# An output projection moved behind eight expert products on TensorE

## The chip, the cores and the metric

The kernel runs on one core of one Trainium2 chip. The metric is the device time of one execution in microseconds (us). Engines are named TensorE (PE in the rows), VectorE (DVE), ScalarE (ACT), GpSimd (POOL) and SyncE (SP); PEld is TensorE's loading of weights.

## What is computed

One layer over 512 tokens of width 1024, float32: a token mixer, then a mixture of single-neuron experts (PEER). The change lies where the one ends and the other begins. Cut to that:

```python
out = jnp.concatenate([y_conv, y_rwkv], axis=-1) @ w_out      # output projection
x = x + gt1 * _rmsnorm(out, ng[1])
hc = _modulate(_rmsnorm(x, ng[2]), sh2, sc2)
q = (hc @ wq).reshape(PEER_CHUNK, PEER_HEADS, 2, D_HALF)
s = jnp.einsum('chsd,hskd->chsk', q, subkeys)
vals, idx = lax.top_k(s, PEER_TOPK)
...                                                           # 16 experts for a token and head: ex, sc
g = jax.nn.softmax(sc.astype(jnp.float32), axis=-1)
act = jax.nn.gelu(jnp.einsum('chkd,cd->chk', u[ex], hc), approximate=False)
y = jnp.einsum('chk,chkd->cd', g * act, v[ex])
```

## The kernel before

The 512 tokens are four tiles of 128. For each tile there are 8 heads, and for each head and token 16 experts, so 32 heads in all (g counts them) with 16 products each. The work of a head goes like this. GpSimd gathers, for each expert slot j, the row of u of each token (128 rows of 4 KB) and the row of v into two rings of 8 buffers each (`gather`, L1570). VectorE multiplies each u row with the tokens and sums (the dots, L1908). When all sixteen dots of a head are there, ScalarE takes gelu of them (L1719), and VectorE multiplies with the softmax (`expert_w`, L1925). ScalarE then makes a diagonal matrix of each weight column (`diags`, L1623, 4 buffers), and TensorE adds diagonal times v row into two PSUM banks (`experts`, L1968, two matmuls of 512 columns, each of which has two records in the trace). The products of head g - 1 are made while the dots of head g run. Between the dots VectorE also chooses the experts of the next head.

The order on each engine is written out by hand in the body of `pool6`, `scalar6`, `vector6` and `tensor6`, and semaphores tie the engines. What sets it around the change:

- GpSimd gathers u row j of head g, then v row j of head g - 1, in turn. U row j waits until the dot that used its buffer 8 slots before is done (`dots`), v row j until the product that used its buffer is done (`experts_added`). A gather that waits holds back all behind it. In head 1 of tile 0 the v rows 8 to 15 of head 0 are gathered beside u rows 8 to 15 of head 1.
- TensorE in tile 0, head 1: after `mixer_moved` reaches 1, eight products of head 0; `project_out(3, 0)`, the output projection of token tile 3 into banks 0 and 1 (L553, 16 matmuls); eight more products. In head 2: `columns(1)`, `columns(2)` (L1437, transposes of the normed rows of tile 1 and 2 into banks 0 and 1; `columns(1)` waits for `mixer_moved` 3), the products of head 1, `columns(3)`. From head 3 on, queries and scores of the later tiles (`late_query` L1989, `late_scores` L1997) stand between the products.
- ScalarE in tile 0, head 1: diagonals 0 to 3, `square_outputs(2)` (L1308 to L1314: it moves the projection out of the banks, takes the sum of squares and a root, and raises `mixer_moved`), diagonals 4 to 7, `square_rows(2)` (L1319), diagonals 8 to 11, `square_outputs(3)`, diagonals 12 to 15; then `exps` (L1645) and gelu. In head 2: the staging of scores (L1616), `square_rows(3)`, `move_columns(1)`, `move_columns(2)` (L1329), the diagonals of head 1, `move_columns(3)`.
- VectorE: `norm_outputs(3)` (L1334 to L1340) stands behind the last dot of head 1 and waits for the root that `square_outputs(3)` makes. Behind it is the wait for gelu.
- SyncE: when all four projections are done (`mixer_output` 4) it loads the first two slices of wq, 1 MB each, for the late queries.

Of the kernel before, what the change touches and what calls it, by code (L numbers as in the profile page):

```python
# [71 lines left out]
def _layer(nc, stack, x, c, ctx_in, c_ctx, w_mod, b_mod, norm_gains, w_in, w_out, conv_w, tshift_mu,  # L72
# [224 lines left out]
    def v3(a):  # L297
        return a.rearrange("p (i c) -> p i c", c=P)
# [1227 lines left out]
    NSL = TOPK  # L1526
# [21 lines left out]
    def late_head(t, h):  # L1548

        if not isinstance(t, int) or t > 1:  # L1550
            return None
        n = h - 3 if t == 0 else h + 5
        return n if 0 <= n < HEADS else None
# [56 lines left out]
    def scalar6(act):  # L1610

        def stage_scores(t, h):

            g = t * HEADS + h
            first = isinstance(t, int) and t == 0
            nc.scalar.activation(SCs[:, h % 2], SC0[:, 2 * h:2 * h + 2, :] if first else SC[:, t, 2 * h:2 * h + 2, :],  # L1616
                                 ACT.Identity).then_inc(scores_staged, 1)

        def diags(g, hp, js):
            for j in js:  # L1620
                if not (isinstance(g, int) and g == 0 and j < 4):
                    act.wait_ge(experts_added, NSL * g + j - 3)
                nc.scalar.activation(diag[:, j % 4], ident, ACT.Identity, scale=expert_w[:, hp % 2, j:j + 1]).then_inc(weight_diagonals, 1)  # L1623

        def last_diagonals():

            act.wait_ge(expert_weights, LAST_HEAD + 1)
            for k, j in enumerate(MULTIPLIED):
                act.wait_ge(experts_added, NSL * LAST_HEAD + k - 3)
                nc.scalar.activation(diag[:, k % 4], ident, ACT.Identity,  # L1630
                                     scale=expert_w[:, LAST_HEAD % 2, j:j + 1]).then_inc(weight_diagonals, 1)

        def finish_last():
            t = NT - 1
            nc.scalar.activation(final_stats[:, 5:6], eps[:, 0:1], ACT.Sqrt)
            act.wait_ge(experts_added, PRODUCTS)
            nc.scalar.activation(tail_squares, psum_all[:, 6 * 512:8 * 512], ACT.Square, accum_out=final_stats[:, 0:1]).then_inc(final_scalar, 1)
            act.wait_ge(final_scalar, 3 * t + 1)
            nc.scalar.activation(final_stats[:, 3:4], final_stats[:, 0:1], ACT.Sqrt, bias=eps[:, 0:1], scale=1.0 / D).then_inc(final_scalar, 1)

        def exps(g):

            act.wait_ge(experts_chosen, g + 1)
            act.wait_ge(probabilities, 2 * g)
            nc.scalar.activation(prob, top, ACT.Exp, bias=neg_largest[:, 0:1], accum_out=exp_sum[:, 0:1]).then_inc(probabilities_raised, 1)  # L1645

        def finish(t):

            act.wait_ge(experts_added, NSL * HEADS * (t + 1))
            act.wait_ge(final_vector, 4 * t + 4)  # L1650
            nc.scalar.activation(square_dump[:, 0:512], PO[0][:, :], ACT.Square, accum_out=final_stats[:, 0:1]).then_inc(final_scalar, 1)
            act.wait_ge(final_scalar, 3 * t + 1)
            nc.scalar.activation(square_dump[:, 0:512], PO[1][:, :], ACT.Square, accum_out=final_stats[:, 1:2]).then_inc(final_scalar, 1)
            act.wait_ge(final_vector, 4 * t + 5)
            nc.scalar.activation(final_stats[:, 3:4], final_stats[:, 2:3], ACT.Sqrt, bias=eps[:, 0:1], scale=1.0 / D).then_inc(final_scalar, 1)


        def late_query(i):

            act.wait_ge(late_queries, i + 1)  # L1660
            nc.scalar.activation(qB[:, i % 2], LATE_QUERY_BANKS[i % 2][:, 0:3 * P], ACT.Identity).then_inc(late_queries_moved, 1)

        def late_scores(i):

            act.wait_ge(late_scores_done, i + 1)
            nc.scalar.activation(SC[:, 1:NT, i, :], v3(LATE_SCORE_BANKS[i % 2][:, 0:3 * P]), ACT.Identity).then_inc(late_scores_moved, 1)

        def body(t, first):
            for h in range(HEADS):
                g = t * HEADS + h  # L1670
                if h == 0 and not first:
                    act.wait_ge(dots, NSL * g)
                    nc.scalar.activation(h2cur, H2N[:, t, :], ACT.Identity).then_inc(h2_current, 1)
                late = late_head(t, h)
                act.wait_ge(experts_chosen, g + 1)
                if first and h < HEADS - 2:
                    act.wait_ge(scores_moved, h + 1)
                elif first:
                    act.wait_ge(late_scores_moved, 2 * (h + 2 - HEADS) + 2)
                elif isinstance(t, int):  # L1680
                    act.wait_ge(late_scores_moved, min(2 * h + 6, 2 * HEADS))
                if h < HEADS - 2:
                    stage_scores(t, h + 2)
                elif t + 1 < NT:
                    stage_scores(t + 1, h + 2 - HEADS)
                if first and h == 1:
                    square_rows(act, 1)
                    act.wait_ge(expert_weights, 1)
                    diags(0, 0, range(4))
                    square_outputs(act, 2, 0)  # L1690
                    diags(0, 0, range(4, 8))
                    square_rows(act, 2)
                    diags(0, 0, range(8, 12))
                    square_outputs(act, 3, 0)
                    diags(0, 0, range(12, NSL))
                elif first and h == 2:
                    square_rows(act, 3)
                    move_columns(act, 1)
                    move_columns(act, 2)
                    act.wait_ge(expert_weights, 2)  # L1700
                    diags(1, 1, range(NSL))
                    move_columns(act, 3)
                elif late is not None:
                    act.wait_ge(expert_weights, g)
                    diags(g - 1, (h - 1) % HEADS, range(6))
                    late_query(2 * late)
                    diags(g - 1, (h - 1) % HEADS, range(6, 13))
                    late_scores(2 * late)
                    late_query(2 * late + 1)
                    diags(g - 1, (h - 1) % HEADS, range(13, NSL))  # L1710
                    late_scores(2 * late + 1)
                elif h or not first:
                    act.wait_ge(expert_weights, g)
                    diags(g - 1, (h - 1) % HEADS, range(NSL))

                if g + 1 < NT * HEADS:
                    exps(g + 1)
                act.wait_ge(dots, NSL * (g + 1))
                nc.scalar.activation(gelu_dot[:, h % 2], acts[:, h % 2], ACT.Gelu).then_inc(gelus, 1)  # L1719
                if h == 0 and not first:  # L1720
                    finish(t - 1)

        def tail():
            last_diagonals()
            finish_last()
        tiles6(act, body, tail)
# [234 lines left out]
    def tensor6(pe):  # L1961
# [39 lines left out]
        def body(t, first):  # L2001
            for h in range(HEADS):
                g = t * HEADS + h
                late = late_head(t, h)
                if h == 1 and not first:
                    pe.wait_ge(final_vector, 4 * t + 4)
                if first and h == 0:
                    continue
                elif first and h == 1:
                    pe.wait_ge(mixer_moved, 1)  # L2010
                    experts(0, 0, range(8))
                    pe.wait_ge(mixer_moved, 2)
                    project_out(3, 0)
                    experts(0, 0, range(8, NSL))
                elif first and h == 2:
                    columns(1)
                    columns(2)
                    experts(1, 1, range(NSL))
                    columns(3)
                elif late is not None:  # L2020
                    experts(g - 1, (h - 1) % HEADS, range(2))
                    late_query(2 * late)
                    experts(g - 1, (h - 1) % HEADS, range(2, 9))
                    late_scores(2 * late)
                    late_query(2 * late + 1)
                    experts(g - 1, (h - 1) % HEADS, range(9, NSL))
                    late_scores(2 * late + 1)
                else:
                    experts(g - 1, (h - 1) % HEADS, range(NSL))
# [650 lines left out]
```

## Time and profile before

| | us |
|---|---|
| median of 3 runs | 2140.48 |
| lowest and highest | 2136.06 and 2141.0 |
| the profiled execution | 2134.94 |
| its span | 2133.3 |
| TensorE busy | 1811.4 (85%) |
| VectorE busy | 1378.9 (65%) |
| GpSimd busy | 1183.5 (55%) |
| ScalarE busy | 647.4 (30%) |

The chain that ended last is TensorE for 46% of the span, DMA for 20%, GpSimd for 13%. A profile row gives a start, a length, the engine, the source line and operation, what is written and read, and how many instructions were merged; in brackets is the idle time before it, and what ended that. The mean granted clock of TensorE was 0.978 of full speed.

### The profile page before, as it was taken

What the parts mean: (1) busy time and instruction counts of PE and PEld (TensorE: products, weight loads), DVE (VectorE), ACT (ScalarE), POOL (GpSimd) and SP (SyncE); (2) the same over time, 40 slices, a digit from 0 to 9 for tenths busy, and PEclk for the clock granted to TensorE, in tenths of its full rate; (3) what the DMA queues carried; (4) which work ended last, traced back from release to release, by engine and by line L of the source; (5) the groups of instructions that cost most, each with busy time, mean ns of one, the idle gap of its engine ahead of it and who ended that gap; (6) DMA issues with size and microseconds to landing.
All of it is one profiled execution on the core that took longest, in us unless ns stands there. A gap on an engine that the chain in (4) does not pass through costs nothing.

```text
span 2133.3 us, 21588 instructions
## 1 busy us (share of the span) xinstructions
PE 1811.4 (85%) x6378; PEld 955.8 (45%) x6378; DVE 1378.9 (65%) x3520; ACT 647.4 (30%) x1510; POOL 1183.5 (55%) x1543
## 2 busy tenths in 40 slices
PE   7999899999998898889988987777777777777776
PEld 2554446999997653444444432222222222222222
DVE  1269863678777597556665567666766665776654
ACT  3145512355453333222222232222222222222221
POOL 2100012454555276766665677776777777677773
PEclk9999999999999999999999999999999999999999
DMA  7354354454455699999999999999999999999997
GB/s 247 93 172 171 107 172 101 123 142 120 121 142 170 210 397 381 406 390 392 381 376 356 369 399 410 409 409 410 409 409 409 410 409 409 399 409 409 409 409 259
DMA packets 295261, 657.34 MB, mean 308 GB/s; under 512 B 71568, under 2 KB 141296, under 8 KB 295152
## 3 DMA queue, kind: packets, MB, share of 16 engines
q0 software_dynamic: 150336, 552.67, 65.8%
q1 hardware_dynamic: 144816, 103.36, 16.5%
q8 instruction: 51, 0.84, 0.2%
q14 instruction: 58, 0.48, 0.1%
HBM read 633.40 MB, written 22.54 MB: 307 GB/s over the span
## 4 chain that ended last, share of the span: by engine, by line
PE 46%; DMA 20%; POOL 13%; DVE 10%; issue 7%; ACT 3%; SPq 1%; DVEq 0%; POOLq 0%; ACTq 0%
PE banks L1968 16%; DMA arena<-in_peer_v_dram,arena 15%; POOL arena L1570 13%; PE banks L2637 4%; PE banks L1989 4%; DMA arena<-in_peer_u_dram,arena 4%; PE banks L553 2%; PE banks L2552 2%; PE banks L1468 1%; PE banks L1057 1%; DVE arena L1908 1%; PE banks L1092 1%; PE banks L1173 1%; PE banks L1096 1%; PE banks L1158 1%
## 5 line engine op out<-in xcount | busy, mean ns | idle before, releaser
L1968 PE MATMUL banks<-arena 128*128 128x512 f32 x1984 | 959.7, 619 | 256.4 <-DMA arena<-in_peer_v_dram,arena 191.0
L1908 DVE CUSTOM_DVE_ANT_0 arena<-arena,banks 128x1024 f32<-128x1024 f32 x512 | 621.1, 1219 | 323.5 <-DMA arena<-in_peer_u_dram,arena 323.3
L1968 PEld LDWEIGHTS banks<-arena 128*128 128x128 f32 x1984 | 359.5, 194 | 843.5 <-issue 450.6
L1570 POOL DMA_INDIRECT arena<-in_peer_v_dram,arena x504 | 472.0, 937 | 238.3 <-PE banks L1968 122.7
L1570 POOL DMA_INDIRECT arena<-in_peer_u_dram,arena x512 | 481.2, 940 | 185.4 <-issue 135.8
L1623 ACT ACTIVATE arena<-arena 128x128 f32<-128x128 f32 x496 | 190.6, 400 | 722.4 <-PE banks L1968 721.6
L2552 PE MATMUL banks<-arena 128*128 128x512 f32 x224 | 109.1, 593 | 0.8 <-ACT arena L2222 0.7
L2637 PE MATMUL banks<-arena 128*128 128x512 f32 x192 | 85.4, 604 | 5.8 <-issue 5.8
L760 POOL TENSOR_TENSOR arena<-arena 128x512 f32<-128x512 f32 x48 | 52.4, 1123 | 65.6 <-issue 50.0
L1989 PE MATMUL banks<-arena 128*128 128x384 f32 x256 | 85.4, 485 | 0.0
L1925 DVE TENSOR_TENSOR arena<-arena 128x16 f32<-128x16 f32 x32 | 5.7, 177 | 123.2 <-ACT arena L1719 123.2
L2169 POOL DMA_DIRECT2D bk_scratch<-arena x8 | 4.3, 533 | 113.1 <-DVE arena L2418 113.1
L1989 PEld LDWEIGHTS banks<-arena 128*128 128x128 f32 x256 | 47.8, 189 | 34.5 <-issue 4.4
L2165 POOL DMA_DIRECT2D vs_scratch<-arena x4 | 2.3, 585 | 109.5 <-ACT arena L2281 109.5
L727 POOL TENSOR_TENSOR arena<-arena 64x256 f32<-64x256 f32 x12 | 7.6, 636 | 97.6 <-DMA arena<-tri_scratch 97.6
L2637 PEld LDWEIGHTS banks<-arena 128*128 128x128 f32 x192 | 36.7, 193 | 51.7 <-issue 51.7
L925 DVE SCALAR_TENSOR_TENSOR arena<-banks,arena 64x64 f32<-64x64 f32 x176 | 49.7, 283 | 15.5 <-PE banks L1041 12.5
L553 PE MATMUL banks<-arena 128*128 128x512 f32 x128 | 57.1, 593 | 0.0
L2552 PEld LDWEIGHTS banks<-arena 128*128 128x128 f32 x224 | 42.0, 189 | 24.9 <-issue 19.5
L898 DVE TENSOR_TENSOR arena<-banks,arena 128x128 f32<-128x128 f32 x96 | 25.8, 287 | 41.5 <-PE banks L1027 41.3
L733 POOL TENSOR_TENSOR arena<-arena 64x14 f32<-64x14 f32 (+6 forms) x168 | 44.5, 265 | 13.2
L731 POOL TENSOR_TENSOR arena<-arena 64x14 f32<-64x14 f32 (+6 forms) x168 | 43.9, 261 | 13.2
(338 smaller groups left out, 2510.2 us busy)
## 6 DMA issues: line engine op xcount, KB each, us to landing
arena<-in_w_mod_dram SPq DMA_DIRECT2D x18, 1024.0 KB, 6.9
arena<-in_peer_wq_dram SPq DMA_DIRECT2D x16, 1024.0 KB, 13.1
arena<-in_w_in_dram SPq DMA_DIRECT2D x27, 512.0 KB, 4.2
arena<-kr_scratch SPq DMA_DIRECT2D x96, 128.0 KB, 3.6
arena<-in_peer_u_dram,arena POOLq DMA_INDIRECT x512, 12.7
arena<-in_peer_v_dram,arena POOLq DMA_INDIRECT x512, 12.9
arena<-in_w_mod_dram SPq DMA_DIRECT2D x3, 2048.0 KB, 12.4
bk_scratch<-arena POOLq DMA_DIRECT2D x8, 768.0 KB, 3.7
```

The source lines that it names most:

```text
L553: m = nc.tensor.matmul(psum[bank + h][:, :], a, wo[:, k, 512 * h:512 * h + 512], start=k == 0, stop=k == KT - 1)
L731: step(nc.gpsimd.tensor_tensor(t, tri[:, 0:j, j:j + 1].broadcast_to([8 * 2 * NB, j, w]), inv[:, j:j + 1, j + 1:SUB].broadcast_to([8 * 2 * ...
L733: step(nc.gpsimd.tensor_tensor(inv[:, 0:j, j + 1:SUB], inv[:, 0:j, j + 1:SUB], t, ALU.add))
L760: nc.gpsimd.tensor_tensor(dst[:, d].rearrange("p i (a b) -> p i a b", b=SUB), src, own, ALU.mult).then_inc(base_spread, 1)
L925: last = nc.vector.scalar_tensor_tensor(dst[rows, cols], C2[d][rows, cols], pc_all[rows, 2 * cp + d, c:c + 1], TMPS[rows, d, cols], ALU.mu ...
L1570: pool.indirect_dma_start(ring[:, j % RING, :], None, table, bass.IndirectOffsetOnAxis(ap=idx[:, hi % 4, j:j + 1].bitcast(U32), axis=0)).t ...
L1623: nc.scalar.activation(diag[:, j % 4], ident, ACT.Identity, scale=expert_w[:, hp % 2, j:j + 1]).then_inc(weight_diagonals, 1)
L1908: nc.vector.tensor_tensor_reduce(u_ring[:, j % RING, :], u_ring[:, j % RING, :], h2cur, 1.0, 0.0, ALU.mult, ALU.add, acts[:, h % 2, j:j + ...
L1968: m = nc.tensor.matmul(PO[h][:, :], diag[:, j % 4], v_ring[:, j % RING, 512 * h:512 * h + 512], start=hp == 0 and j == 0, stop=hp == HEADS ...
L1989: m = nc.tensor.matmul(LATE_QUERY_BANKS[i % 2][:, 0:3 * P], wq2[i // 2 % 2][:, k, a:a + P], h2T[:, k], start=k == 0, stop=k == KT - 1)
L2552: m = nc.tensor.matmul(psum[bx][:, 0:T], wring[:, j, k, :], hT[:, k, TC:TT], start=k == 0, stop=k == KT - 1)
L2637: m = nc.tensor.matmul(psum[CONV_BANKS[q][j]][:, 0:T], wring[:, j, k, :], hT[:, k, TC:TT], start=k == 0, stop=k == KT - 1)
```

## The change

TensorE does all sixteen products of head 0 at once, with `project_out(3, 0)` behind them. ScalarE makes the diagonals 8 to 15 in one go, with `square_outputs(3)` behind them.

```diff
@@ scalar6, body, head 1 of tile 0
                     square_rows(act, 2)
-                    diags(0, 0, range(8, 12))
+                    diags(0, 0, range(8, NSL))
                     square_outputs(act, 3, 0)
-                    diags(0, 0, range(12, NSL))
                 elif first and h == 2:
@@ tensor6, body, head 1 of tile 0
                     pe.wait_ge(mixer_moved, 1)
-                    experts(0, 0, range(8))
+                    experts(0, 0, range(NSL))
                     pe.wait_ge(mixer_moved, 2)
                     project_out(3, 0)
-                    experts(0, 0, range(8, NSL))
                 elif first and h == 2:
```

## Rows read from the trace of the kernel before

**Rows 1.** Timeline of TensorE: start, length, operation; idle before it in brackets.
```profile
779.07 13.92 PE L1968 MATMUL banks<-arena 128*128 128x512 f32 x32
792.83 13.90 PE L553 MATMUL banks<-arena 128*128 128x512 f32 x32
806.56 13.92 PE L1968 MATMUL banks<-arena 128*128 128x512 f32 x32
...
824.27 17.73 PE L1968 MATMUL banks<-arena 128*128 128x512 f32 x40 [1.03 <-ACT arena L1623]
...
856.43 1.96 PE L1968 MATMUL banks<-arena 128*128 128x512 f32 x4 [0.60 <-DMA arena<-in_peer_v_dram,arena]
...
863.92 5.82 PE L1968 MATMUL banks<-arena 128*128 128x512 f32 x8 [4.66 <-ACT arena L1623]
...
909.97 6.68 PE L1968 MATMUL banks<-arena 128*128 128x512 f32 x8 [4.47 <-ACT arena L1623]
```

**Rows 2.** The chain that ended last, merged: start, length, what.
```profile
847.07 9.23 DMA arena<-in_peer_v_dram,arena
856.43 1.96 PE banks L1968 x4
```

**Rows 3.** Waits of TensorE from 860 to 1240: us in total, times, longest.
```profile
PE banks L1968 <- ACT arena L1623: 32.4, 7, 5.4
```

**Rows 4.** Stretches: length, busy us of PE, PEld, DVE, ACT, POOL, granted clock, DMA share, GB/s.
```profile
862.00:864.00 2.00, 0.08 (x1) 0.08 (x1) 0.78 (x4) 1.99 (x5) 1.69 (x2) 0.50 1.03 414
...
1300.00:1400.00 100.00, 76.37 (x156) 26.44 (x156) 66.89 (x192) 25.49 (x58) 75.58 (x81) 1.00 1.03 409
```

**Rows 5.** Timeline of ScalarE.
```profile
792.72 1.26 ACT L1623 ACTIVATE arena<-arena 128x128 f32<-128x128 f32 x4
806.76 1.02 ACT L1308 ACTIVATE arena<-banks 128x1024 f32<-128x1024 f32 x1 [12.77 <-PE banks L553]
...
809.11 0.39 ACT L1623 ACTIVATE arena<-arena 128x128 f32<-128x128 f32 x1
...
814.06 1.28 ACT L1645 ACT_TABLE_LOAD   x1
...
817.50 1.04 ACT L1319 ACTIVATE arena<-arena 128x1024 f32<-128x1024 f32 x1
...
820.96 1.09 ACT L1329 ACTIVATE arena<-banks 128x512 f32<-128x512 f32 x2 [0.72 <-PE banks L1437]
...
823.82 1.27 ACT L1623 ACTIVATE arena<-arena 128x128 f32<-128x128 f32 x4
```

**Rows 6.** Timeline of GpSimd: first and last v row of head 0's second half, then the next.
```profile
781.22 0.93 POOL L1570 DMA_INDIRECT arena<-in_peer_v_dram,arena  x1 [3.00 <-PE banks L1968]
...
798.64 0.93 POOL L1570 DMA_INDIRECT arena<-in_peer_v_dram,arena  x1 [0.30 <-DVE arena L1908]
799.87 0.94 POOL L1570 DMA_INDIRECT arena<-in_peer_u_dram,arena  x1 [0.30 <-issue]
808.71 0.94 POOL L1570 DMA_INDIRECT arena<-in_peer_v_dram,arena  x1 [7.90 <-PE banks L1968]
```

**Rows 7.** DMA issues in 781:782, 798.5:799.5, 806:808: queue, count, median us to landing.
```profile
arena<-in_peer_v_dram,arena POOLq DMA_INDIRECT x1, 5.1
...
arena<-in_peer_v_dram,arena POOLq DMA_INDIRECT x1, 7.0
...
arena<-in_peer_wq_dram SPq DMA_DIRECT2D x2, 1024.0 KB, 8.5
```

**Rows 8.** Timeline of VectorE: last dot of head 1, first dot of head 2.
```profile
807.87 1.22 DVE L1908 CUSTOM_DVE_ANT_0 arena<-arena,banks 128x1024 f32<-128x1024 f32 x1
...
817.80 1.21 DVE L1908 CUSTOM_DVE_ANT_0 arena<-arena,banks 128x1024 f32<-128x1024 f32 x1
```

## The prediction

> **What bounds the kernel now.** I read the chain of waits first, then the stretch around the change engine by engine. Times are us from the span's start; (h, j) is expert j of head h of tile 0. The changed stretch lies where TensorE is the bound: from 779 to 820 it runs without a stop, eight products of head 0 (L1968), project_out(3) (L553), eight more products [rows 1]. The merged row of eight products is 13.76 us from its start to the next row's, so a product is 1.72; the projection takes 13.73. From 824.27 TensorE works on head 1; its last product starts at 856.43 [rows 1], and in the chain that one is released by a v row issued at 847.07 which took 9.23 to land [rows 2]: the bound has passed to GpSimd and DMA. So the sixteen products of head 1 take 32.16 from first start to last, where 15 x 1.72 = 25.8 would do: 6.4 us of slack, which will matter. From head 2 on until about 1240 TensorE waits only for ScalarE's diagonals, 7 times [rows 3]: a shift of TensorE at the start of head 2, now 863.92 [rows 1], goes whole into that stretch. After it DMA is full: share 1.03, 409 GB/s from 1300 to 1400 [rows 4]; nothing is won back there. The sum is therefore one number: how much later (2, 0) starts.
>
> **What the change does.** No instruction is added or removed. On TensorE project_out(3) moves behind (0, 8) to (0, 15); on ScalarE the diagonals 12 to 15 come before square_outputs(3).
>
> Part one, the eight products. Their first needs diagonal 8. ScalarE makes it at 792.72 [rows 5] in both kernels, after square_rows(2). A diagonal begun at 823.82 [rows 5] released a product at 824.27 [rows 1], 0.45 later, so (0, 8) starts at 793.17 instead of at 792.83: 0.34 lost. Their v rows must now be there 13.7 us sooner than before. They are issued between 781.22 and 798.64, in seven steps of 2.49 [rows 6], and land 5.1 (first) to 7.0 (last) later [rows 7]; the last is there at 805.64 and can be used 0.13 later (847.07 + 9.23 = 856.30 against the start at 856.43 [rows 1, 2]). Without a stop (0, 15) would start at 793.17 + 7 x 1.72 = 805.21; it starts at 805.77. The products end at 807.49, the projection at 821.22.
>
> Part two, what is behind the projection on ScalarE. Square_outputs(3) starts 0.20 after the projection ends (806.76 [rows 5] after 806.56 [rows 1]), so at 821.42: 14.66 later. ScalarE has the last four diagonals behind it now, from 809.11 to 814.06 [rows 5]; they move ahead, into time when it is idle, and that saves 4.95. So exps, gelu and square_rows(3) are later by 14.66 - 4.95 = 9.71: square_rows(3) starts at 827.21 instead of 817.50. Move_columns(1) starts 0.72 after ScalarE was free (it waited for TensorE [rows 5]), a wait that falls away, since columns(1) runs on TensorE near 824. Hence 820.96 - 0.72 + 9.71 = 829.95, and from there 3.31 to (1, 0) (820.96 to 824.27 [rows 1, 5]): (1, 0) starts at 833.26, **8.99 later**. In the 12 us between TensorE has only the transposes of columns(1) and columns(2).
>
> Part three, VectorE. It ends the dots of head 1 at 807.87 + 1.22 = 809.1 [rows 8], then waits in norm_outputs(3) for square_outputs(3), and behind that for gelu. Its first dot of head 2 moves with gelu by 9.71, from 817.80 [rows 8] to 827.51.
>
> Part four, the gathers. GpSimd stops now for 7.90 before the v row at 808.71 [rows 6], which waits for (0, 8). In the changed kernel (0, 8) ends at 794.9 and this stop is gone: the row goes out at 801.1, 7.6 earlier. It cannot keep that. Sixteen gathers after the u row at 799.87 [rows 6], at about 799.87 + 8 x 2.49 = 819.8, it comes to u row 8 of head 2, which needs that first dot: stop until about 828.9 (827.51 + 1.22 and a little). The next gather, v row 8 of head 1, needs (1, 0). Both are in one queue, so the later u rows wait as well. SyncE's two 1 MB loads of wq, which wait for the projection, are issued in 806 to 808 now [rows 7] and will be at 821.4, into a DMA that runs empty; they have until 869, so they cost nothing, and they no longer stand beside the gathers.
>
> Part five, TensorE's clock. After the stop of 4.66 before 863.92 the first two products took 5.82, and after the similar one before 909.97 they took 6.68 [rows 1]; full speed is 3.44. The granted clock stood at 0.50 in 862 to 864 [rows 4]: 1.2 of 2.4 GHz. The longer stop before 833.26 is new, and at 824.27 there was no such loss. I take the middle, 6.25 for (1, 0) and (1, 1); the bounds are 3.44 (no loss) and 6.68.
>
> Then (1, 1) ends at 839.51. GpSimd follows a product's end by 0.43 (779.07 + 1.72 to 781.22 [rows 1, 6]), so v row 9 is issued at 839.94, v row 15 six steps of 2.49 later at 854.88. A landing costs between 7.0, as after the earlier stop, and the 9.2 of before; I take 7.0 [rows 7], since this sequence starts like that one, with a drained queue. (1, 15) starts at 854.88 + 7.0 + 0.13 = 862.0. By TensorE alone it would be 839.51 + 13 x 1.72 = 861.9: both limits meet. Against 856.43 that is **+5.6 us**, and what stands between (1, 15) and (2, 0), columns(3) and ScalarE's exps, gelu and diagonal, is unchanged.
>
> The Trainium skill, TensorE: Matmul & The Clock Gate, section "What's actually happening", says of the slow start that for modelling it is under 1% of a typical span and is not to be fitted. By that rule part five would be nothing and the sum +3.5. The rows at 863.92 and 909.97 speak for pricing it here, since the whole effect is a fraction of a per cent.
>
> **Sum.** Bounds of the mechanism: with no clock loss (1, 0) ends at 834.98, v row 8 is issued at 835.4, row 15 at 852.8, (1, 15) starts at 860.0: +3.5. With 6.68 and landings of 9.2: v row 15 at 855.3, start at 864.7: +8.2. The profiled execution took 2134.94 (span 2133.3), 5.5 below the median of 2140.48. It would become 2140.5; the median becomes 2146.1.
>
> **The rivals.**
> - A, the above: +5.6, 2146.1 us. Chance 0.46, of which 0.12 lies past +6.4 us. That is 0.3%, about what a measurement of this kernel can tell from no change.
> - B, no slack takes it up: gathers land as late as before (9.2) or slower, or the u rows stopped with the v rows hold head 2's dots back, and the 9.0 of (1, 0) plus the clock's 2.8 arrive whole: +8.2 to +11.8, about 2150. For it: the chain has that v row at 9.23 [rows 2]. Against: that latency was a queue built up, with 2 MB of wq in it. 0.27.
> - C, the restart costs no clock: +3.5, 2144.0. The page named above would have it so. For: between 820.3 and 824.27 it had only transposes too, and ten products then took 17.73, full speed. Against: the two other rows [rows 1]. 0.08.
> - D, the delay is taken up later or the stop at 821 is shorter: within 2 us of before, 2141. For: GpSimd gains 7.6 at 801. Against: TensorE's stops in heads 2 to 8 are all ScalarE's [rows 3]. 0.13.
> - E, faster: GpSimd's stop of 7.90 is gone and the lead of 7.6 lasts. Its place is the gather at 819.8, the point that decides whether the first dot of head 2 ends by then: 2132.9. Against: that dot waits behind gelu, itself behind the projection, at 827.5. 0.06.
> - That the change does not do what it says, because the v rows of (0, 8) to (0, 15) are not there: with all landings at 9.2, (0, 15) starts at 808.0, 2.2 later, and all behind it too. It lies inside B.
>
> **The numbers.** Slower by over 0.3%: 0.12 + 0.27 = 0.39, and with a little of C and D 0.40. Within 0.3%: 0.34 of A and nearly all of C and D, 0.54. Faster: 0.06. The range leaves out E and the tail of B: 2139 to 2152.
>
> **What would show it.** Right: the projection's row of TensorE ends near 821; a stop of some 12 us on TensorE before (1, 0) near 833, which ScalarE's diagonal ends; a first pair of products of about 6 us; no stop of GpSimd at 808 but two stops, about 820 to 829 for VectorE and 830 to 837 for TensorE; (2, 0) near 869.5. Wrong: (1, 0) before 830, or (2, 0) at 864 or at 873, or a distance from (2, 0) to the end that is other than now.

## The result, and the profile after

Measured beside the kernel before on one chip: median 2144.99 us against 2138.91, 20 runs of each. The ratio is 1.0031, 95% interval 1.0023 to 1.0039, so the changed kernel is slower by 6.6 us, with 4.9 to 8.3 inside the interval. (The ratio is not the quotient of the medians; these differ by 6.1.) The forecast was +5.6 us and 2146.1, the range 2139 to 2152.

In the table (h, j) is the product of expert j of head h of tile 0, as in the prediction.

| | before | after |
|---|---|---|
| median, us | 2138.91 | 2144.99 |
| profiled execution | 2134.94 | 2147.54 |
| its span | 2133.3 | 2145.9 |
| (0, 0) starts | 779.07 | 784.68 |
| (0, 0) to (1, 0) | 45.20 | 55.97 |
| (0, 0) to (2, 0) | 84.85 | 92.25 |
| (2, 0) to the end of the span | 1269.4 | 1269.0 |

The two profiled executions lie 12.6 us apart, twice the effect. 5.6 of it is there at (0, 0), where the two kernels have done the same work. The medians do not show it (see cols_here and the paragraph behind it). So times are read from (0, 0): the stretch grew by 7.4, and what is behind it is as long as before.

TensorE after the change. The lines of the file are one lower from here on: L1967 are the products, L1437 the columns' transposes. These rows answer to [rows 1].

```profile
784.68 13.92 PE L1967 MATMUL banks<-arena 128*128 128x512 f32 x32
799.53 12.31 PE L1967 MATMUL banks<-arena 128*128 128x512 f32 x28 [0.93 <-ACT arena L1623]
812.26 1.96 PE L1967 MATMUL banks<-arena 128*128 128x512 f32 x4 [0.42 <-DMA arena<-in_peer_v_dram,arena]
814.05 13.90 PE L553 MATMUL banks<-arena 128*128 128x512 f32 x32
830.21 1.06 PE L1437 MATMUL banks<-arena 128*128 128x128 f32 x8 [2.25 <-ACTq L431]
837.74 1.94 PE L1437 MATMUL banks<-arena 128*128 128x128 f32 x8 [6.47 <-ACT arena L1329]
840.65 30.78 PE L1967 MATMUL banks<-arena 128*128 128x512 f32 x64 [0.97 <-ACT arena L1623]
871.27 1.03 PE L1437 MATMUL banks<-arena 128*128 128x128 f32 x8
876.93 5.40 PE L1967 MATMUL banks<-arena 128*128 128x512 f32 x8 [4.62 <-ACT arena L1623]
```

Before the second half of head 0's products TensorE stops for 0.93, for its first diagonal, and inside it for 0.42, for its last v row. Behind the projection there are 12.9 us in which TensorE has only transposes. Then the sixteen products of head 1 run without a wait: the stops for v rows before the last of them [rows 1] are gone, and TensorE is the limit there.

ScalarE, the chain that releases head 1 (answers to [rows 5]):

```profile
827.99 1.02 ACT L1308 ACTIVATE arena<-banks 128x1024 f32<-128x1024 f32 x1 [20.87 <-PE banks L553]
...
830.45 1.28 ACT L1645 ACT_TABLE_LOAD   x1
...
833.88 1.04 ACT L1319 ACTIVATE arena<-arena 128x1024 f32<-128x1024 f32 x1
...
836.53 1.07 ACT L1329 ACTIVATE arena<-banks 128x512 f32<-128x512 f32 x2
...
840.21 1.27 ACT L1623 ACTIVATE arena<-arena 128x128 f32<-128x128 f32 x4
```

ScalarE sits idle for 20.87 and then has square_outputs(3), exps, gelu, square_rows(3) and the moves in one row. TensorE has nothing but the transposes of columns(1) and columns(2) beside them.

GpSimd (answers to [rows 6]) and VectorE:

```profile
825.68 0.93 POOL L1570 DMA_INDIRECT arena<-in_peer_v_dram,arena  x1 [0.31 <-issue]
835.68 0.94 POOL L1570 DMA_INDIRECT arena<-in_peer_u_dram,arena  x1 [9.06 <-DVE arena L1907]
844.71 0.94 POOL L1570 DMA_INDIRECT arena<-in_peer_v_dram,arena  x1 [8.09 <-PE banks L1967]
```

```profile
830.46 0.16 DVE L1334 RECIPROCAL arena<-arena 128x1 f32<-128x1 f32 x1 [14.99 <-ACT arena L1314]
```

GpSimd's stop of 7.90 is gone [rows 6]. In its place there are two, 9.06 for VectorE's first dot of head 2 and 8.09 for (1, 0). VectorE itself stands still for 14.99 in norm_outputs(3).

Stretches of 2 us (columns as in [rows 4]):

```profile
838.00:840.00 2.00, 1.68 (x8) 1.27 (x6) 1.96 (x9) 0.89 (x2) 0.00 (x0) 0.50 0.55 219
840.00:842.00 2.00, 1.35 (x2) 0.83 (x3) 1.97 (x15) 1.47 (x5) 0.00 (x0) 0.50 0.00 0
842.00:844.00 2.00, 2.00 (x3) 0.68 (x3) 1.97 (x13) 0.00 (x0) 0.00 (x0) 0.50 0.00 0
```

TensorE's granted clock is 0.50, 1.2 of 2.4 GHz, after the stop behind the projection. From 840 to 844 DMA moves nothing, in a kernel that later is bound by DMA.

### The profile page after: what moved, and what is told of

It reads as the page before. It is cut to its first block, busy times and chain, and to the rows that moved or that the text cites. A ratio compares the mean times of both kernels' runs of the same rounds, so it can differ in the third digit from the quotient of the medians.

```text
span 2145.9 us, 21588 instructions
## 1 busy us (share of the span) xinstructions
PE 1814.7 (85%) x6378; PEld 958.4 (45%) x6378; DVE 1378.6 (64%) x3520; ACT 647.5 (30%) x1510; POOL 1186.1 (55%) x1543
## 4 chain that ended last, share of the span: by engine, by line
PE 23%; DMA 19%; POOL 13%; issue 6%; DVE 5%; ACT 3%; POOLq 0%; ACTq 0%; DVEq 0%
PE banks L1967 16%; DMA arena<-in_peer_v_dram,arena 15%; POOL arena L1570 13%; DMA arena<-in_peer_u_dram,arena 5%; PE banks L1988 4%; DVE arena L1907 2%; PE banks L553 1%; ACT L1718 1%; ACT L1645 1%; PE banks L1996 1%; PE banks L2035 0%; POOL arena L1605 0%; DVE arena L1879 0%; PE banks L1173 0%; PE banks L1143 0%
## 5 line engine op out<-in xcount | busy, mean ns | idle before, releaser
L1967 PE MATMUL banks<-arena 128*128 128x512 f32 x1984 | 960.9, 620 | 253.0 <-DMA arena<-in_peer_v_dram,arena 189.0
L1967 PEld LDWEIGHTS banks<-arena 128*128 128x128 f32 x1984 | 360.8, 195 | 840.3 <-issue 448.0
```

The lines of the kernel that those rows point to most:

```text
L1967: m = nc.tensor.matmul(PO[h][:, :], diag[:, j % 4], v_ring[:, j % RING, 512 * h:512 * h + 512], start=hp == 0 and j == 0, stop=hp == HEADS ...
```

## The experiments

The theories, as the expectations number them. **1**: the loss is the projection's: it ends 14.7 us later, and ScalarE's work behind it releases head 1. **2**: ScalarE's new order costs. **3**: v rows wanted too early. **4**: VectorE's stop, and the u rows behind it. **5**, which came with the last four runs: head 1's products, when they start at once, free the v buffers sooner, which pays only on a slower chip. The first eight kernels ran on one chip, the last four on another.

**again.** The changed kernel, no edit.

> The changed kernel once more, beside the others on one chip. If its loss is real, about +6 us against the kernel before (ratio near 1.003). Its first profile entered the stretch 5.6 us later than the kernel before had; if that is chance, the distance from the first to the last product of the stretch repeats here (first product of head 0 to first of head 2: 92.2 us, before 84.9) while the entry moves. If the late entry belongs to the change, it repeats too.

2256.94 us against 2251.33 for the kernel before, ratio 1.0018 (0.9996 to 1.0041). This chip is slower for both kernels, by some 5%, its mean granted clock is lower (0.91 to 0.93 against 0.97 to 0.98), and its runs scatter more (before: 2240.77 to 2265.41), so a ratio here is good to about 0.2%. The size agrees with +6, but does not show a loss by itself. The distance from (0, 0) to (2, 0) was 107.8 us, not the 92.2 that was expected; on the faster chip it is 91.2 (after_here). The trace shows ScalarE stopped for 11.6 us at once with no engine of this core named as the cause:

```profile
ACT arena L1329 <- remote: 13.1, 2, 11.6
```

**act_order.** ScalarE's part alone.

```diff
-                    diags(0, 0, range(8, 12))
+                    diags(0, 0, range(8, NSL))
                     square_outputs(act, 3, 0)
-                    diags(0, 0, range(12, NSL))
```

> The kernel before with ScalarE's part of the change alone: diagonals 8 to 15 in one go, square_outputs(3) behind them; TensorE keeps 8, projection, 8. Theory 1 (the loss comes from the projection being done 14.7 us later, and ScalarE's work behind it): square_outputs(3) starts some 7 us later, gelu and the first product of head 1 some 2 us later, which the 6.4 us of slack in head 1 take up: 0 us, ratio 1.000. Theory 2 (ScalarE's new order is itself what costs): the same +6 us as the whole change.

Ratio 1.0007 (0.9984 to 1.0030), median 2251.43 against 2251.33. No loss is seen, as theory 1 had it, but theory 2 is not excluded by this run: its +6 us is 1.0027, just inside the interval. Nor can this ratio be told from again's 1.0018.

**split12.** The projection moved half as far.

```diff
-                    experts(0, 0, range(8))
+                    experts(0, 0, range(12))
                     pe.wait_ge(mixer_moved, 2)
                     project_out(3, 0)
-                    experts(0, 0, range(8, NSL))
+                    experts(0, 0, range(12, NSL))
```

> The kernel before with the projection moved half as far: 12 products, projection, 4 products; ScalarE's order as before. Theory 1: the projection ends 6.9 to 7.2 us later, (1, 0) starts 6.5 later, of which the slack takes most: +1.5 us, with a slow clock after the new stop +3. Theory 3 (what costs is that the v rows of the second half are wanted early, so that TensorE stands before them): nothing, since rows 8 to 11 land in time; 0 us.

Ratio 1.0012 (0.9994 to 1.0031). It lies between the kernel before and the changed one, but 0 and +3 us are both inside: inconclusive.

**warm.** The changed kernel with nine more matmuls of 512 columns, whose result is not used, so that TensorE's clock does not fall.

```diff
+        def keep_warm(n):
+            for _ in range(n):
+                nc.tensor.matmul(psum[2][:, :], ident, wo[:, 0, 0:512], start=True, stop=True)
 tensor6, head 2 of tile 0:
+                    keep_warm(2)
                     columns(1)
+                    keep_warm(7)
                     columns(2)
```

> The changed kernel with nine 512-column matmuls whose results nobody uses, in TensorE's stop between the projection and head 1 (two before columns(1), seven before columns(2)). Work is added, only the clock should change. Theory 1 with the clock's term: columns(2) takes 1.06 instead of 1.94 and head 1's first products run at full speed; v row 8 is issued about 3 us earlier, and the time is 3 us under the changed kernel's, about +3 to +4 against before. If the clock's loss were hidden behind the v rows: no gain, +6.

Timeline of TensorE, first of warm, then of again:

```profile
847.33 1.06 PE L1437 MATMUL banks<-arena 128*128 128x128 f32 x8 [0.45 <-ACT arena L1329]
849.42 26.36 PE L1967 MATMUL banks<-arena 128*128 128x512 f32 x60 [1.03 <-ACT arena L1623]
```

```profile
851.79 1.94 PE L1437 MATMUL banks<-arena 128*128 128x128 f32 x8 [5.95 <-ACT arena L1329]
854.71 27.83 PE L1967 MATMUL banks<-arena 128*128 128x512 f32 x60 [0.98 <-ACT arena L1623]
```

So columns(2) is a term of the clock too: 1.94 without the added work and 1.06 with it. The first fifteen products of head 1 are 1.47 faster. The time, however, was not: the ratio is 1.0023 (1.0000 to 1.0046), not below again's. The expected 3 us are 0.13%, less than either interval can tell. Whether these 2.4 us reach the end is not shown; on this chip other waits, such as the one above, stand between (1, 15) and (2, 0) (18.02 us before (2, 0) in warm, 13.64 in again).

**gelu_early.** The changed kernel, VectorE set free. `weights_of(1, 1)` holds exps(2), the wait for the dots and the gelu of head 1, which stood behind square_outputs(3).

```diff
 scalar6, head 1 of tile 0:
                     diags(0, 0, range(8, NSL))
+                    weights_of(1, 1)
                     square_outputs(act, 3, 0)
 vector6:
-                    elif first and (h, j) == (1, NSL - 1):
+                    elif first and (h, j) == (2, 5):
                         norm_outputs(dve, 3)
-                    elif first and (h, j) == (2, 5):
+                    elif first and (h, j) == (2, 9):
                         norm_rows(dve, 3)
```

> The changed kernel with exps and gelu of head 1 ahead of square_outputs(3) on ScalarE, and norm_outputs(3) and norm_rows(3) later among VectorE's dots (after dots 5 and 9 of head 2). VectorE is no longer stopped for 15 us, and u row 8 is not held. Head 1's products still come behind square_outputs(3), square_rows(3) and the two column moves. Theory 1: (1, 0) and v row 8 are as late as in the changed kernel: +5 to +7 us. Theory 4 (the loss is VectorE's stop and the u rows behind it): it falls to about 0.

Ratio 1.0044 (1.0022 to 1.0065): the loss is all there, and theory 4, which had it fall to about 0, is refuted. GpSimd's two stops have become one, before v row 8 of head 1, and TensorE is the one it waits for (shorter ones put down to remote aside):

```profile
860.34 0.94 POOL L1570 DMA_INDIRECT arena<-in_peer_v_dram,arena  x1 [16.84 <-PE banks L1973]
```

**after_cols_later.** The changed kernel, head 1's products ahead of the columns.

```diff
 tensor6, head 2 of tile 0:
-                    columns(1)
-                    columns(2)
-                    experts(1, 1, range(NSL))
+                    experts(1, 1, range(4))
+                    columns(1)
+                    experts(1, 1, range(4, 8))
+                    columns(2)
+                    experts(1, 1, range(8, NSL))
                     columns(3)
 scalar6, head 2 of tile 0:
-                    square_rows(act, 3)
-                    move_columns(act, 1)
-                    move_columns(act, 2)
                     act.wait_ge(expert_weights, 2)
-                    diags(1, 1, range(NSL))
+                    diags(1, 1, range(4))
+                    diags(1, 1, range(4, 8))
+                    move_columns(act, 1)
+                    square_rows(act, 3)
+                    diags(1, 1, range(8, 12))
+                    move_columns(act, 2)
+                    diags(1, 1, range(12, NSL))
                     move_columns(act, 3)
```

> The changed kernel with head 1's products ahead of the columns: TensorE does (1, 0) to (1, 3), columns(1), four products, columns(2), the rest; ScalarE makes the diagonals in that order, square_rows(3) among them. VectorE's stop stays. Theory 1: (1, 0) starts about 28 us instead of 34 us behind the end of the second half of head 0's products, less what the chain of square_rows(3) and the moves took: about 5 us earlier than in the changed kernel; time +1 to +3 against before. Theory 4: no change from the changed kernel, +6.

Ratio 0.9972 (0.9953 to 0.9992), 6 us under the kernel before. The changed one stood at 1.0018, so about 10 us came back, more than the 3 to 5 that were expected; the two ratios are of different comparisons. Theory 4, which had no change here, falls again.

**cols_later.** The same edit on the kernel before.

> The kernel before with the same move of head 1's products ahead of the columns, projection where it was. TensorE loses its 4 us of stops at 820 to 824, but v row 8 of head 1 goes out behind GpSimd's stop of 7.9 us at about 829 all the same, and the v rows end head 1. Theory 1: 0 us, ratio 1.000 (within 0.1%). If TensorE were the limit at the end of head 1: -4 us.

Ratio 0.9968 (0.9949 to 0.9988): -7 us where 0 was expected. On this chip theory 1's bookkeeping of what limits the end of head 1 is not the right one, and after_cols_later's 10 us are not the lost 4 alone: the larger part is this gain. What the pair does show: with head 1's products ahead of the columns the moved projection costs nothing that can be seen (medians 2247.86 with it, 2247.92 without, each good to about 0.2%).

**both.** The edits of gelu_early and after_cols_later together; ScalarE makes diagonals 0 to 3 of head 1 ahead of square_outputs(3).

> The changed kernel with both: gelu of head 1 ahead of square_outputs(3), and head 1's products ahead of the columns, so that (1, 0) starts right behind the projection. GpSimd keeps its lead of 7.6 us, v row 8 goes out about 823 instead of 829, and the first stop is gone too. Theory 1: head 1 ends some 7 us sooner than in the kernel before: -7 us, ratio 0.997. If the placement of the sixteen products has a cost of its own (v rows, DMA), 0 or more.

Ratio 0.9942 (0.9923 to 0.9960), -13 us, 6 below cols_later, as expected of the step between the two; the -7 us expected against the kernel before was missed by cols_later's 7.

**before_here.** The kernel before, no edit, for a trace beside the next three.

> The kernel before, unchanged, for a trace of it from the same chip as the others of this call. The chip of the eight runs so far is some 5% slower (2251 against 2139 us) and moves some 370 GB/s in the gathers instead of 409; there cols_later gained 7 us where 0 was expected. Theory 1: on such a chip (2, 0) comes more than 84.9 us after (0, 0), and the surplus is in DMA. Ratio 1.000.

This was another chip, and it takes 2139 us again: median 2138.98, ratio 1.0005 (0.9995 to 1.0015). (0, 0) starts at 780.26, (2, 0) at 863.93, 83.7 us later. What was expected of the slower chip could not be seen here.

**after_here.** The changed kernel, no edit.

> The changed kernel beside it. Theory 1: +4 to +7 us; the distance from (0, 0) to (2, 0) grows by as much, and what comes behind (2, 0) is as long as before.

2145.69 us, ratio 1.0031 (1.0019 to 1.0043): the loss again, and by this interval a loss for certain. (0, 0) at 784.70, (2, 0) at 875.91, so 91.2, which is 7.5 more; behind it 1268.4 against 1269.6. These are (0, 0), (1, 0) and (2, 0), first in before_here (the second row ends at the edge of the window asked for), then in after_here:

```profile
780.26 13.92 PE L1968 MATMUL banks<-arena 128*128 128x512 f32 x32
...
825.48 5.00 PE L1968 MATMUL banks<-arena 128*128 128x512 f32 x11 [1.03 <-ACT arena L1623]
...
863.93 6.00 PE L1968 MATMUL banks<-arena 128*128 128x512 f32 x8 [4.63 <-ACT arena L1623]
```

```profile
784.70 13.92 PE L1967 MATMUL banks<-arena 128*128 128x512 f32 x32
...
839.94 30.47 PE L1967 MATMUL banks<-arena 128*128 128x512 f32 x64 [0.98 <-ACT arena L1623]
...
875.91 5.40 PE L1967 MATMUL banks<-arena 128*128 128x512 f32 x8 [4.63 <-ACT arena L1623]
```

**cols_here.** As cols_later.

> cols_later beside them. Theory 5: starting head 1's products at once frees the v buffers sooner and with it the gathers behind them, which pays where DMA is slow or stops (-7 us) and not where the v rows arrive on GpSimd's own beat (0 us on a chip that takes 2139 us). The trace tells: v row 8 of head 1 waits for (1, 0) in the kernel before and not here.

Ratio 1.0000 (0.9989 to 1.0011). (0, 0) to (2, 0) takes 84.9. GpSimd's stop before v row 0 of head 1 is as in the kernel before [rows 6]:

```profile
816.19 0.94 POOL L1570 DMA_INDIRECT arena<-in_peer_v_dram,arena  x1 [7.69 <-PE banks L1971]
```

So on this chip theory 1's 0 us holds. The 4 us of transposes and stops that TensorE has between its products of head 0 and head 1 [rows 1] were worth nothing. Nor does v row 8 of head 1 wait for (1, 0) in before_here (830.56, 0.30 idle before it), which fits theory 5's 0 for this chip.

The run also bears on the late entry. Here (0, 0) starts at 786.54, 6.3 us later than in before_here, while the medians are equal (2138.87 and 2138.98). The two profiled executions, 2141.15 and 2135.10, lie 2.3 above and 3.9 below their medians, which is that difference: between these two kernels the entry differs by the execution. For the changed kernel the same is not shown so plainly. Its late entry did come again, at 784.70 in after_here, and of the six traces from chips that take 2139 us both of the kernel before are early (779.07, 780.26) and all four of edited kernels late (784.68 to 786.54). What speaks against counting it to the change is the time: the spans of the two pairs differ by 12.6 and 10.8 us, the medians by only 6.1 and 6.7. Either way it stands apart from the 7.4 and 7.5 of the stretch.

**both_here.** As both.

> both beside them. Theory 1: 6 to 7 us under cols_here, whatever the chip, since GpSimd's stop before v row 0 of head 1 is gone: -7 us against before on a chip that takes 2139, -13 on the slower one.

2135.13 us, ratio 0.9989 (0.9979 to 1.0000): -2.4 us, not -7. (The medians, 2135.13 and 2138.42, differ by 3.3.) It is the fastest of the kernels on either chip, if by little on this one. Its TensorE has no stop between the projection and head 1, and GpSimd has one of 1.52 there, before v row 8 (the last row of TensorE ends at the edge of the window):

```profile
813.81 13.90 PE L553 MATMUL banks<-arena 128*128 128x512 f32 x32
827.54 7.04 PE L1976 MATMUL banks<-arena 128*128 128x512 f32 x16
...
859.26 1.96 PE L1976 MATMUL banks<-arena 128*128 128x512 f32 x4 [0.59 <-DMA arena<-in_peer_v_dram,arena]
...
866.72 3.65 PE L1976 MATMUL banks<-arena 128*128 128x512 f32 x4 [4.63 <-ACT arena L1623]
```

```profile
829.70 0.94 POOL L1570 DMA_INDIRECT arena<-in_peer_v_dram,arena  x1 [1.52 <-PE banks L1976]
```

From (0, 0), v row 8 goes out at 45.0 instead of 50.3 (830.56 - 780.26 in before_here), 5.3 sooner. But (1, 15) starts at 74.5 instead of 76.2, only 1.7 sooner. Between the two is the queue: v rows issued late in head 1 take longer to land. Those issued in before_here from 845 to 850, then one issued in both_here from 848.8 to 849.6:

```profile
arena<-in_peer_v_dram,arena POOLq DMA_INDIRECT x2, 8.2
```

```profile
arena<-in_peer_v_dram,arena POOLq DMA_INDIRECT x1, 10.1
```

Part of that is SyncE's 2 MB of wq. In before_here they are issued into the stop of GpSimd and land 8.7 us later; in both_here they are issued behind the later projection, among the gathers, take 20.7, and hold a quarter of the DMA time from 845 to 850, where before_here has gathers alone:

```profile
q1 hardware_dynamic: 416, 0.42, 24.2%
```

The stretches of 2 us in before_here show what there was to win:

```profile
806.00:808.00 2.00, 2.00 (x6) 0.94 (x5) 2.00 (x4) 0.04 (x1) 0.00 (x0) 1.00 0.35 141
808.00:810.00 2.00, 2.00 (x6) 0.85 (x5) 2.00 (x5) 1.99 (x3) 0.09 (x1) 1.00 0.31 62
```

A full DMA has a share of 1.03, so these 4 us hold (0.68 + 0.72) x 2 = 2.8 us of missing transfer. By this account that, and not the 7.6 us of GpSimd's stop, bounds the gain of removing the stop. The measured -2.4 (interval -4.5 to 0) and the -1.7 in the trace agree with 2.8 and exclude 7; one pair of kernels does not show it to be a rule.

What stays open is the slower chip: why the columns' order gave 7 us there. The traces say where it lies. From (0, 0) to (2, 0) it took 86.6 us in cols_later, 94.9 in after_cols_later and 88.3 in both, against 98.2 in act_order and 104 to 108 in again, split12, warm and gelu_early, one execution of each. Theory 5's sign, a v row 8 that waits for (1, 0) in the kernel before, can't be read, since no trace of that kernel exists from that chip. act_order has such a wait (8.08 us), but its ScalarE runs later.

## Why the prediction was right, and where its working was off

The direction, the mechanism and nearly the size were right; 2144.99 is in the range, 1.1 under the forecast, and the loss by the ratio is 1.0 over the forecast one. The median lies under the forecast although the loss lies over it, because the forecast started from three runs of the kernel before (2140.48), and twenty give 2138.91. By the traces the stretch grew by 7.4 and 7.5, 1.8 and 1.9 over the forecast, so the times flatter the working a little. The forecast gave 0.54 to a change within 0.3% and 0.40 to a larger loss; with 0.31% and an interval of 0.23 to 0.39 the result sits on that line. Against the traces, all counted from (0, 0):

| | forecast | after | after_here |
|---|---|---|---|
| (0, 8) starts | 14.1 | 14.85 | 14.39 |
| projection starts | 28.4 | 29.4 | 28.6 |
| (1, 0) starts | 54.2 | 55.97 | 55.24 |
| (2, 0) later than before by | +5.6 | +7.4 | +7.5 |

**Part one** had two stops, for diagonal 8 and for v row 15, at 0.34 and about 0.6. They were 0.93 and 0.42 in one execution, and 0.47 and 0.16 in the other. The first hangs on square_rows(2), which hangs on VectorE; it is the part that moves from execution to execution.

**Part two** was the core and holds. From projection's end to (1, 0) the forecast had 12.04; it was 12.9 in both executions (827.79 to 840.65, 827.07 to 839.94). Up to move_columns(1) it is exact: 8.73 behind the projection's end by forecast, 8.74 in the trace (836.53). What fails is the sentence in it that takes 3.31 from there to (1, 0) as in the kernel before; it was 4.12. Columns(2) lies in this piece and now ran at 1.2 GHz: 1.94 instead of 1.06. The clock was charged to the products in part five and not to the transposes before them.

**Part three** happened (a stop of 14.99). In gelu_early, without it, the loss stayed, so it is not what the loss hangs on while (1, 0) is as late.

**Part four** was right in kind: the stop at 808 gone, two new ones of 9.06 and 8.09, and DMA empty by the end of the second. The landing of 7.0 was right too; four rows of the changed kernel around v row 15 have it:

```profile
arena<-in_peer_v_dram,arena POOLq DMA_INDIRECT x2, 7.0
arena<-in_peer_u_dram,arena POOLq DMA_INDIRECT x2, 7.0
```

**Part five** put the clock's loss at 2.81 us. The sixteen products took 30.62 (840.65 to 871.27) and 30.31, against 27.5 at full speed: 3.1 and 2.8. The sum had both limits meet at (1, 15), and they nearly did: v row 15, issued at 862.66, was there 6.5 later, 0.4 before its product, so TensorE was the limit by that much. From (1, 0) to (2, 0) the forecast had 36.2 and the trace has 36.3. The 1.8 that the stretch missed are therefore all there at (1, 0), in two terms of TensorE that were mis-sized: 0.9 for the clock of columns(2), and 0.9 for the stops of part one. In after_here (1, 0) is 1.05 later than forecast, 0.9 and 0.2 by the same terms; the growth is 7.5 all the same, since the stretch of before_here is 1.2 shorter than that of the kernel before had been.

The Trainium skill, TensorE: Matmul & The Clock Gate, section "What's actually happening", says that for modelling the slow start costs under 1% of a typical kernel span and that no specific cold count is to be fitted. This case's rows agree with the 1%: 3 us of 2139 are 0.14%. Left out of the sum, though, as the prediction read it, the term gives +3.5, below the interval of 4.9 to 8.3, since here 3 us are half the effect. That the time falls by them when the clock is kept up is not shown; warm tried it and could not resolve it.

**The rivals.** B, with +8.2 and more, is above the measured +6.6, though its low end still lies in the interval (up to 8.3). The traces decide against it: it had nothing take up the delay, and 10.8 at (1, 0) had become 7.4 at (2, 0). C's full clock did not come. D's absorption did not either: (2, 0) to the end is 1269.4 and 1269.0. E, the lead of 7.6 that lasts, did not come in the changed kernel; it is what the kernel both builds. It was worth 2.4 on the faster chip, so E's price was wrong as well: it took GpSimd's idle time for time gained, where by the account above only DMA's idle time counts.

## What to carry to other kernels

When a block of work is moved behind others on one engine, follow what other engines do with its result. The new order cost TensorE itself only 0.6 to 1.4 us of stops among its products; what made head 1 late was five steps of ScalarE behind the projection, which were once hidden beside eight products and now stood alone. If the late consumer also frees buffers for a full DMA queue, the queue runs dry; and before a stall of the issuing engine is taken for time to be won, look how far the DMA share falls in it: here 7.6 us of stall held 2.8 us of missing transfer. Where a stop is new, charge the slow clock to everything behind it, the small transposes too.

## What the runs showed of the hardware

One chip took 2251 us for what two measurements elsewhere took 2139 for. Between 1300 and 1400 its DMA moved 377 GB/s in act_order (409 in [rows 4]), and TensorE's granted clock there was 0.90 instead of 1.00; which of the two is cause and which is consequence is not shown:

```profile
1300.00:1400.00 100.00, 67.14 (x133) 25.81 (x134) 61.35 (x172) 19.17 (x45) 65.42 (x71) 0.90 0.98 377
```

An edit that gave 0.0% on the faster chip gave -0.32% on it. A result of a few tenths of a per cent on one chip need not hold on the next.
